# The expert layer of a decoder trunk: weights loaded as 7168-byte rows of one side at a time, in place of 3584-byte rows of gate and up in turn

## The reference, cut to what matters

```python
D_MODEL, SEQ, N_EXPERTS, TOP_K, D_FF_EXPERT = 1024, 256, 8, 2, 3584

def swiglu(h, w_gate, w_up, w_down):
    return (jax.nn.silu(h @ w_gate) * (h @ w_up)) @ w_down

def moe_swiglu(h, router_w, w_gate, w_up, w_down):
    logits = (tokens @ router_w).astype(jnp.float32)
    top_vals, top_idx = lax.top_k(logits, TOP_K)
    top_w = jax.nn.softmax(top_vals, axis=-1)
    combine = jnp.sum(jax.nn.one_hot(top_idx, N_EXPERTS) * top_w[..., None], axis=1)
    out = jnp.zeros_like(tokens)
    for e in range(N_EXPERTS):
        y = swiglu(tokens, w_gate[e], w_up[e], w_down[e])
        out = out + combine[:, e:e + 1] * y
```

## Time and profile before

| | us |
|---|---|
| median of three runs | 2023.57 |
| the profiled execution | 2022.8 |
| its span in the profile | 2021.0 |
| first hidden product of the first pass | 1154.81 |
| first hidden product of the second pass | 1261.51 |
| last down product of the last pass ends | 2007.45 |
| last store issued | 2016.67 |

### The profile page before, as it was taken

How to read it: one execution, slowest core, us unless ns; L and a number is a source line. 1 busy time by engine, 2 the same in 40 slices (tenths; PEclk the granted TensorE clock), 3 DMA queues, 4 the chain that set the end, 5 groups by cost and what they waited for, 6 DMA issues and landing times.

```text
span 2021.0 us, 67888 instructions
## 1 busy us (share of the span) xinstructions
PE 1945.3 (96%) x31760; PEld 1723.7 (85%) x31760; DVE 391.4 (19%) x945; ACT 273.1 (14%) x580; POOL 87.9 (4%) x174
## 2 busy tenths in 40 slices
PE   7999999999999999999999899999999999999997
PEld 7888888888777688888888799989998998989897
DVE  3335331110000133533311301001010001010001
ACT  1223214000000122222310000000000000000001
POOL 4010101000000001011000000000000000000000
PEclk9999999999999999999999899999999999999999
DMA  8413123467442141311346499999999999999996
GB/s 243 126 43 105 44 80 110 146 207 251 144 148 86 40 150 62 104 44 44 120 131 221 148 391 407 407 407 408 407 407 407 407 407 407 407 407 407 408 407 264
DMA packets 214765, 483.01 MB, mean 239 GB/s; under 512 B 11582, under 2 KB 110092, under 8 KB 214668
## 3 DMA queue, kind: packets, MB, share of 16 engines
q1 hardware_dynamic: 214668, 481.54, 64.0%
HBM read 480.46 MB, written 1.05 MB: 238 GB/s over the span
## 4 chain that ended last, share of the span: by engine, by line
PE 83%; DMA 6%; SPq 4%; DVE 3%; ACT 1%; issue 1%; POOL 0%; DVEq 0%; ACTq 0%
PE bank L640 32%; PE bank L627 18%; PE bank L1167 7%; DMA pool<-in_moe_w_down_dram 6%; PE bank L732 5%; PE bank L1090 4%; PE bank L1127 4%; SPq L2154 3%; PE bank L1106 3%; PE bank L688 2%; PE bank L1315 1%; SPq L2159 1%; PE bank L1053 1%; DVE pool L1834 0%; PE bank L1013 0%
## 5 line engine op out<-in xcount | busy, mean ns | idle before, releaser
L640 PE MATMUL bank<-pool 128*64 128x80 f32 x21504 | 757.6, 234 | 34.6 <-DMA pool<-in_moe_w_down_dram 26.8
L640 PEld LDWEIGHTS bank<-pool 128*64 128x64 f32 x21504 | 752.3, 138 | 41.3 <-DMA pool<-in_moe_w_down_dram 28.9
L627 PE MATMUL bank<-hnT,pool 128*128 128x256 f32 x1856 | 428.1, 384 | 0.4 <-DVE pool L1896 0.4
L627 PEld LDWEIGHTS bank<-hnT,pool 128*128 128x128 f32 x1856 | 346.5, 190 | 55.2 <-issue 8.8
L1167 PEld LDWEIGHTS bank<-hnT,pool 128*128 128x128 f32 x640 | 121.6, 190 | 23.3 <-issue 7.7
L1167 PE MATMUL bank<-hnT,pool 128*128 128x256 f32 x640 | 140.7, 379 | 0.0
L2054 DVE TENSOR_TENSOR pool<-pool,bank 128x320 f32<-128x320 f32 x32 | 15.6, 488 | 642.7 <-ACT pool L1601 642.7
L732 PEld LDWEIGHTS bank<-pool 64*64 64x64 f32 x3008 | 94.8, 135 | 17.2 <-issue 11.2
L1601 ACT ACTIVATE pool<-bank 128x320 f32<-128x320 f32 x32 | 14.0, 437 | 692.7 <-PE bank L640 692.7
L732 PE MATMUL bank<-pool 64*64 64x32 f32 (+2 forms) x3008 | 103.4, 221 | 2.6 <-DVE pool L1680 1.6
L565 POOL TENSOR_TENSOR pool<-pool,level_mask 128x256 f32<-128x256 f32 x72 | 51.9, 735 | 775.1 <-DVE pool L1756 495.1
(11 more groups left out here) (320 smaller groups left out, 1175.9 us busy)
## 6 DMA issues: line engine op xcount, KB each, us to landing
pool<-in_moe_w_up_dram SPq DMA_DIRECT2D x128, 896.0 KB, 16.6
pool<-in_moe_w_gate_dram SPq DMA_DIRECT2D x128, 896.0 KB, 16.6
pool<-in_w_in_dram SPq DMA_DIRECT2D x66, 1024.0 KB, 5.3
pool<-in_moe_w_down_dram SPq DMA_DIRECT2D x64, 1024.0 KB, 16.8
pool<-in_moe_w_down_dram SPq DMA_DIRECT2D x32, 1536.0 KB, 18.6
pool<-in_ffn_w_gate_dram SPq DMA_DIRECT2D x11, 1024.0 KB, 7.6
pool<-in_ffn_w_up_dram SPq DMA_DIRECT2D x11, 1024.0 KB, 5.5
pool<-in_ffn_w_down_dram SPq DMA_DIRECT2D x11, 1024.0 KB, 5.0
```

The lines of the kernel that those rows point to most:

```text
L627: ins = mm(ps[:, s * T:(s + 1) * T], w[:, k, (j + s) * P:(j + s + 1) * P], hnT[:, k, :], start=(k == 0), stop=(k == KD - 1))
L640: ins = mm(bank[rows, cs], w[:, rows], rhs, start=start, stop=stop, skip_group_check=True)
```

## The change

A pass becomes 2 halves (NH) of 14 tiles (HT) in place of 4 rounds of 7. In a half, TensorE first goes through all of gate, eight slots, then through all of up in the same eight slots, then through down in two rounds of 7 tiles. A hidden slot now holds one k-tile by 14 tiles of one matrix: 1792 floats as before, but 128 rows of 7168 bytes. The 14 tiles lie in four parts of 4, 3, 4 and 3 tiles (PARTS) in the four banks B[2], B[3], proj[0], proj[1]. Gate fills them; ScalarE takes silu of each into the buffer sge, now twice as large; up then fills the same banks, and VectorE multiplies sge by them into heT, which still holds 7 tiles, so parts 2 and 3 are multiplied only once down's first round has read parts 0 and 1. One semaphore, hid_free, counts both ScalarE's and VectorE's releases. Down has six slots (DSLOTS), five of one tile and one of two. The wait of TensorE for the residual adds (sc_added) moves from the first round to ahead of the zero matmuls.

The order of SP's queue in a pass is written in one_pass: up of half 0; gate of half 1, slots 0 and 1; down round 1; gate of half 1, slots 2 to 7; up of half 1; down round 2; the next pass's gate, slots 0 and 1; down round 3; the next pass's gate, slots 2 to 7; its down round 0. Ahead of the first pass SP loads down round 0 and gate of half 0.

```diff
-SPLIT = 4
-HSLOT = 2 * FB * P
-KH = 4
+NH = 2
+HT = FT // NH
+HSLOT = HT * P
+PARTS = (range(0, 4), range(4, 7), range(7, 11), range(11, 14))
+DSLOTS = 6
...
-            lo = 2 * KH * HSLOT
-            return pool[:, lo + 2 * n * D:lo + min(2 * n + (3 if n == 2 else 2), FB) * D].rearrange("p (f n) -> p f n", n=D)
-
-        assert 2 * KH * HSLOT + FB * D <= MRING * SLOT
+            lo = KD * HSLOT
+            return pool[:, lo + n * D:lo + (FB if n == DSLOTS - 1 else n + 1) * D].rearrange("p (f n) -> p f n", n=D)
+
+        assert KD * HSLOT + FB * D <= MRING * SLOT and KD + DSLOTS <= MRING
...
+                hidden_banks = (B[2], B[3], proj[0], proj[1])
                 with pe.Fori(0, n_pass) as i:
                     pe.wait_ge(xg_ready, i * 2 + 2)
                     pe.wait_ge(selT_ready, i + 1)
+                    pe.wait_ge(sc_added, i * 4 + 4)
                     for half in range(2):
                         mm(B[4 + half][:, 0:4 * CAP], zeros[:, 0:P], zeros[:, :], start=True, stop=False,
                            skip_group_check=True)
...
+                    with pe.Fori(0, NH) as h:
+
+                        def hidden(side):
+
+                            for n in range(KD):
+                                pe.wait_ge(hid_loaded[n], i * (32 * NH) + h * 32 + side * 16 + 16 * (slot_count[n] + 1))
+                                for q in range(4):
+                                    if n == 0:
+                                        pe.wait_ge(hid_free, i * (8 * NH) + h * 8 + side * 4 + (ff_base + q + 1))
+                                    for f in PARTS[q]:
+                                        at = f - PARTS[q][0]
+                                        ins = columns_mm(hidden_banks[q], slice(at * CAP, (at + 1) * CAP),
+                                                         hidden_slot(n)[:, f * P:(f + 1) * P], xgT[:, n, :],
+                                                         start=(n == 0 and at == 0), stop=(n == KD - 1))
+                                    if n == KD - 1:
+                                        ins.then_inc(hid_mm, 1)
+                                if n < KD - 1:
+                                    ins.then_inc(hid_used, 1)
+
+                        def down(r):
+
+                            for f in range(FB):
+                                if f == PARTS[0][0] or f == PARTS[1][0]:
+                                    pe.wait_ge(hid_free, i * (8 * NH) + h * 8 + r * 2
+                                               + (ff_base + 8 + (1 if f == PARTS[0][0] else 2)))
+                                n, at = min(f, DSLOTS - 1), max(f - (DSLOTS - 1), 0)
                                 if at == 0:
...
+                                    pe.wait_ge(dwn_loaded[n], i * (16 * NR) + h * 32 + r * 16 + 16 * (slot_count[KD + n] + 1))
+                                for k in range(KD):
+                                    ins = columns_mm(B[4 + k // 4], slice(k % 4 * CAP, (k % 4 + 1) * CAP),
+                                                     down_slot(n)[:, at, k * P:(k + 1) * P], heT[:, f, :],
+                                                     start=False, stop=False)
+                                    if f == FB - 1 and k % 4 == 3:
+                                        ins.then_inc(dwn_mm, 1)
+                                if n < DSLOTS - 1:
                                     ins.then_inc(dwn_used, 1)
...
+                        with pe.Fori(0, 2) as side:
+                            hidden(side)
+                        with pe.Fori(0, 2) as r:
+                            down(r)
...
+                for h in range(NH):
+                    for q in range(4):
+                        lo, n = PARTS[q][0], len(PARTS[q])
+                        act.wait_ge(hid_mm, i * (8 * NH) + (hid_base + 8 * h + q + 1))
+                        A(sge[:, lo:lo + n, :], (B[2], B[3], proj[0], proj[1])[q][:, 0:n * CAP].rearrange("p (f n) -> p f n", f=n),
+                          ACT.Silu).then_inc(hid_free, 1)
...
+                    for h in range(NH):
+                        for q in range(4):
+                            lo, n, g = PARTS[q][0], len(PARTS[q]), q % 2
+                            v.wait_ge(hid_mm, i * (8 * NH) + (hid_base + 8 * h + 4 + q + 1))
+                            if q == 2:
+                                v.wait_ge(dwn_used, i * ((DSLOTS - 1) * NR) + ((DSLOTS - 1) * 2 * h + 4))
+                            if q == 3:
+                                v.wait_ge(dwn_mm, i * (2 * NR) + (down_base + 4 * h + 2))
+                            tt(heT[:, PARTS[g][0]:PARTS[g][0] + n, :], sge[:, lo:lo + n, :],
+                               (B[2], B[3], proj[0], proj[1])[q][:, 0:n * CAP].rearrange("p (f n) -> p f n", f=n),
+                               ALU.mult).then_inc(hid_free, 1)
+                        if h == 0:
                             places(i + 1)
...
-            def hidden_load(n, e, col):
-
-                w = (a["moe_w_gate"], a["moe_w_up"])[n % 2]
-                rows = slice(n // 2 * 2 * P, (n // 2 + 1) * 2 * P)
-                src = w[0, e, rows, col].rearrange("a (k p) n -> p (a k) n", p=P)
+            def hidden_load(n, e, side, h):
+
+                w = (a["moe_w_gate"], a["moe_w_up"])[side]
+                src = w[0, e, n * P:(n + 1) * P, h * HSLOT:(h + 1) * HSLOT].rearrange("a p n -> p (a n)")
                 sp_.dma_start(hidden_slot(n), src).then_inc(hid_loaded[n], 16)

-            def down_load(n, e, rows):
-
-                src = a["moe_w_down"][0, e, rows, :].rearrange("a (f p) n -> p (a f) n", p=P)
+            def down_load(n, e, r):
+
+                lo, hi = (r * FB + n) * P, (r * FB + (FB if n == DSLOTS - 1 else n + 1)) * P
+                src = a["moe_w_down"][0, e, lo:hi, :].rearrange("a (f p) n -> p (a f) n", p=P)
                 sp_.dma_start(down_slot(n), src).then_inc(dwn_loaded[n], 16)
...
+            for n in range(DSLOTS):
+                down_load(n, slice(0, 1), 0)
...
+                        hidden_load(n, slice(0, 1), 0, 0)
                         fetched.append(n)
...
-            def later_round(e, col, hid, dwn):
-
-                for n in range(2 * KH):
-                    sp_.wait_ge(hid_used, hid + (n + 1))
-                    hidden_load(n, bass.ds(e, 1), bass.ds(col, FB * P))
-                for n in range(3):
-                    if n < 2:
-                        sp_.wait_ge(dwn_used, dwn + 1)
+            def hidden_round(i, at, e, slots):
+
+                h, side = at // 2 % NH, at % 2
+                for n in slots:
+                    if n < KD - 1:
+                        sp_.wait_ge(hid_used, i * ((KD - 1) * 2 * NH) + ((KD - 1) * (at - 1) + n + 1))
                     else:
-                        sp_.wait_ge(dwn_mm, dwn * 2 + (down_base + 2))
-                    lo, size = down_rows(n)
-                    down_load(n, bass.ds(e, 1), bass.ds(col + lo, size))
-
-            def rest_of_pass(i, e):
-
-                with sp_.Fori(0, NR - 1) as j:
-                    later_round(e, j * (FB * P) + FB * P, i * (2 * KH * NR) + j * (2 * KH), i * NR + j)
+                        sp_.wait_ge(hid_mm, i * (8 * NH) + (hid_base + 4 * at))
+                    hidden_load(n, bass.ds(e, 1), side, h)
+
+            def down_round(i, at, e):
+
+                for n in range(DSLOTS):
+                    if n < DSLOTS - 1:
+                        sp_.wait_ge(dwn_used, i * ((DSLOTS - 1) * NR) + ((DSLOTS - 1) * (at - 1) + n + 1))
+                    else:
+                        sp_.wait_ge(dwn_mm, i * (2 * NR) + (down_base + 2 * at))
+                    down_load(n, bass.ds(e, 1), at % NR)
+
+            def one_pass(i, e, next_e):
+
+                hidden_round(i, 1, e, range(0, KD))
+                hidden_round(i, 2, e, range(0, 2))
+                down_round(i, 1, e)
+                hidden_round(i, 2, e, range(2, KD))
+                hidden_round(i, 3, e, range(0, KD))
+                down_round(i, 2, e)
+                if next_e is not None:
+                    hidden_round(i, 4, next_e, range(0, 2))
+                down_round(i, 3, e)
+                if next_e is not None:
+                    hidden_round(i, 4, next_e, range(2, KD))
+                    down_round(i, 4, next_e)

```

More of the change, by code:

```diff
@@ L2176, in _ @@
                     clear.append(ring)
-                for n in range(2 * KH):
+                for n in range(KD):
                     needs = [r for r in range(RING) if r * SLOT < (n + 1) * HSLOT and n * HSLOT < (r + 1) * SLOT]
                     if n not in fetched and all(r in clear for r in needs):
-                        hidden_load(n, slice(0, 1), slice(0, FB * P))
+                        hidden_load(n, slice(0, 1), 0, 0)
                         fetched.append(n)
-            assert len(fetched) == 2 * KH
+            assert len(fetched) == KD
```

95 lines of the change are left out of this document (9 added, 86 removed).

## The result

The changed kernel takes 2049.9 us (median of 4 runs, 2045.1 to 2052.0) against 2023.5 in the same comparison: ratio 1.0135, 95% interval 1.0118 to 1.0151. It is slower, as forecast, but by three times the forecast, and outside the range (2014 to 2042). The profiled span is 2049.3 us against 2021.0: 28.3 us more, where the sum said 9.2.

A forecast was written before the change was run, and what follows sets the result against it. Transfers were taken to bound the kernel, TensorE having about 6 us of slack a pass. Long rows' gain was outweighed by a 2.5 us stream pause each pass; with the first pass's +4.8 us, +9.2 us gave 2032.8, range 2014 to 2042.

The forecast's parts named there:

- the sum: Whole kernel: first pass +4.8 us, six passes of 109.1 and a last without the next gate's two slots; +9.2 us.
- T0: The end of a pass's last down product, from which the forecast counted both TensorE's work and the transfers.
- The first pass: Its last down product was forecast at 1257.6 against 1252.85 before, +4.8 us, with the queue empty for some 12 us.
- The packet price: Time of one 7168-byte row in the hidden loads, taken as 275 ns, bounds 268 and 281.
- the rival that rows bring nothing: Long rows cut or no better per byte in the hidden loads: +6.0 us more, 2038.8 us; chance 0.13.
- the one that the stream doesn't pause: Long rows pay and the stream doesn't pause: passes of 106.6 us, 2011 us in all; chance 0.13.
- From there the bytes bind to the end of the pass.: After down 1's data start: 35.2 us of hidden slots, 27.15 of tiles, 0.2, 0.5 and 2.23; the pass 109.1 us.
- The 2.1 us from rows 9: Delay from a load's issue into an empty queue until its data in effect flow, read after a pause: 2.1 us.
- The last pass: Taken as a 109.1 us pass less 4.4 us, for the next gate's two slots that it doesn't load.
- The pause itself: Stream dry at T0 + 41.5 until down 1's data at T0 + 43.8: 2.3 us, with another 0.2 following.
- TensorE's leg: From T0 through 16 hidden slots and down 0's first tile until down 1's data flow, loop ends included: 43.8 us.
- TensorE's price for loop ends: Register work of TensorE's loops and waits in a half: 0.3 us a pass, bounds 0 and 1.

The follow-up runs named there:

- e1_gate4: Against the changed kernel, SP's order alone: four slots of the second half's gate, in place of two, go out ahead of down round 1; 2013.9 us.
- e3_rows3584: Against the changed kernel, each hidden load split into two loads of 448 KB with 3584-byte rows; 2062.5 us.
- e7_double: Against the changed kernel, two sets of down slots, down rounds written out, loads in the order slots come free; 2092.8 us.
- e6_unrolled: Against the changed kernel, TensorE's two inner loops (side and round) written out; 2245.5 us.

## Why the prediction was wrong

**What held.** The bound and the mechanism: SP's queue holds six freed gate slots behind down 1, the stream runs dry once a pass, and this costs more than the long rows bring. SP's first load of down 1 was predicted at T0 + 41.7 (43.8 less 2.1); it went out at 1411.91, 41.7 us after 1370.2. That this is exact is partly luck: TensorE took 9.07 us between the passes (8.66 in the sum), and SP issued 0.1 us after the tile was used (0.45 in the sum). The first pass's queue was empty from about 1183 to 1190, where 1180 to 1192 was forecast. The packet price was taken as 275 ns; two microseconds with only long rows have 116 of them beside 12 completions:

```profile
DMA packets 128, 0.83 MB, mean 416 GB/s; under 512 B 12, under 2 KB 12, under 8 KB 128
...
q1 hardware_dynamic: 128, 0.83, 100.3%
```

16 x 2000 / 116 = 276 ns. Full windows have 416 to 421 GB/s, more than the 412 forecast. That speaks against the rival that rows bring nothing; the one that the stream doesn't pause is false by the dip.

**The step that failed** is the one behind the pause: "From there the bytes bind to the end of the pass." It takes the full rate from the first byte of down 1 on, in every pass. It was short in three places, and they make up 19.0 us of the difference of 19.1:

- Passes 2 to 7, 110.84 against 109.07 forecast, +10.6 us. Down 1 was to land 11.9 us after its first issue (2.1 + 9.25 + 0.5). It landed at 1425.4, 13.5 us after: the loads are issued one at a time, as TensorE releases tiles, into an empty queue, which then moves 287 GB/s and not the 405 of a full one. The 2.1 us from rows 9 were taken once, but the queue stays shallow for the whole round. From there on the bytes did bind: down 3's last slot landed 52.8 us after down 1's, where the sum has 53.3, and in between the stream moved 417 GB/s. Told by the stream, the same pass is 104.6 us of transfers and 5.9 us missing, where the sum had 106.6 and 2.5: the pause was sized at less than half, and the faster stream hid 2 us of that.
- The last pass, from the last down product of the pass before to its own, 111.5 against 104.7, +6.9 us. I took off 4.4 us because it doesn't load the next gate. The bytes did not bind (286 GB/s from 2020 to 2031 us); TensorE, its clock and the reload of down's last slot did. The chain of the last pass in the changed kernel:

```profile
1933.28 39.28 PE bank L642 x1120
...
1972.71 7.51 DMA pool<-in_moe_w_down_dram
...
1980.27 43.13 PE bank L642 x1184
...
2023.56 8.00 DMA pool<-in_moe_w_down_dram
...
2031.60 4.08 PE bank L642 x64
```

39.3 us of matmuls, a load of 7.5, 43.1 of matmuls, a load of 8.0, and 64 matmuls at the low clock: no row of the stream's rate in it. The 43.1 us have a low stretch too; the same work takes 42.0 in the other passes. So 2.8 of the 6.9 us are the clock (1.1 and 4.08 less 2.43), by these rows. In e1_gate4, without the pause, the last pass took 108.8 us, and passes 4 to 7 105.7: there too nothing is queued ahead of down 3 in the last pass. The last slot of a down round is loaded only after all of the round before, so it can stand in the chain in each half.
- The first pass ends at 1259.1 against 1257.6, +1.5 us, though its first hidden product starts 0.9 us earlier than before (1153.92). Its timeline:

```profile
1169.47 33.20 PE L642 MATMUL bank<-pool 128*64 128x80 f32 x921 [2.70 <-issue]
1203.81 2.44 PE L642 MATMUL bank<-pool 128*64 128x80 f32 x64 [1.14 <-DMA pool<-in_moe_w_down_dram]
1206.65 39.23 PE L642 MATMUL bank<-pool 128*64 128x80 f32 x1120 [0.41 <-issue]
1249.00 10.10 PE L642 MATMUL bank<-pool 128*64 128x80 f32 x224 [3.12 <-DMA pool<-in_moe_w_down_dram]
```

One issue gap of 2.70 us (2.4 taken), then waits of 1.14 and 3.12 us for down 1 and down 3, the last followed by 10.10 us for 224 matmuls.

The pause itself was also too small: 2.5 us forecast, 5.3 us missing by the windows from 1408 to 1422. Of these 3.8 us lie before 1414.0, where data of down 1 were to flow, and 1.5 behind it, in the slow start just told. The start of down 1's data was right, so the stream ended sooner than T0 + 41.5; it faded from 1409 to 1411. I had counted from the moment when the last down slot of the pass before has landed less 0.5 us. In the records of the changed kernel, 4096-byte packets of that slot and 7168-byte packets of the next load overlap from 1365.0 to 1367.3: the 16 engines are some 2.3 us apart, and while the last of them finish one load, others are already in the next. So the stream was further in the mean than the landing says, by about 1.2 us as an estimate from these rows. No run tests that this is the cause. In the sum this changes nothing, since TensorE's leg sets the start of down 1: the 5.9 us of stream and the late landing are two accounts of one loss. It matters for how much cover a pause needs: four slots, where the forecast pause of 2.5 us would have asked for three or four.

The clock was no term at all. Passes 1 to 7 have a wait of about 3.2 us at down 3 and with it 3.4 or 6.8 us at 1.2 GHz. In passes with 3.4 us the chain goes past it, through the reload of the last down slot; in the two with 6.8 it goes through the slow matmuls. Two pieces of the chain, of passes 3 and 5:

```profile
1467.60 10.65 DMA pool<-in_moe_w_down_dram
...
1691.51 10.79 PE bank L642 x224
```

The two with 6.8 us took 111.3 and 111.7 us. Passes with the same wait for down 1 (1.21 and 1.72 us against 1.25 and 1.70) and 3.4 us of low clock took 110.5 and 111.1, so it adds 0.8 and 0.6 us there. With the 2.8 us of the last pass that is some 4 of the 19.1 us, an estimate from these rows; no run changes the clock alone.

TensorE's price for loop ends was taken at 0.3 us a pass. Its pace went from 34.8 to 35.1 ns (44.92 us for 1280), 0.8 us in 2688, and there is a gap of 0.36 us between halves. On the leg where the 0.3 was used, 928 matmuls took 32.5 us where the sum has 32.3: it was the right order.

The experiments show the order as the cause of the loss: with the same loops, rows, slots and bytes, two numbers in SP's queue are worth 36 us, more than the 26 that the change lost.

## What to carry to other kernels

When one queue feeds two rings of slots, its order fixes how much lies behind the load that has to wait for the slowest release; count the transfers ahead of that load against the time until its slot is free, in both directions: too few and the stream stops, too many and the reader waits, frees its slots late, and the stream stops behind the load. Here the right number was four of eight, one slot to either side costs 16 us, and an edit in one half moved the pause to the other, so the numbers are to be set together. When a change makes the stream faster, look again for what binds: a loop that was bound by bytes, with 6 us to spare on TensorE, became bound in its first half by TensorE and the one load that waits for a whole round, and in the last pass in both halves.

## What the runs showed of the hardware

- A queue that was empty and is fed load by load moved 287 GB/s in windows where full ones move 405 to 421 (changed kernel, 1413 to 1419 us).
- The 16 DMA engines of one stream were about 2.3 us apart (changed kernel, 4096-byte packets of one load and 7168-byte packets of the next overlapping from 1365.0 to 1367.3 us).
- Rows of 7168 bytes ran at 276 ns a packet in a window of 2 us and at 416 to 421 GB/s over full windows (changed kernel), those of 3584 bytes at 405 to 409, in loads of 896 KB (before) and of 448 KB (e3_rows3584) alike.
- Seven waits of TensorE of 3.1 to 3.2 us each came with 3.4 or 6.8 us at 1.2 GHz (changed kernel); of the ten waits of 2.11 to 2.13 us before the change three did.
- TensorE's loop of 672 pairs of weight load and matmul (a half of the changed kernel, a round of the one before) ran with 0.02 MB of code loads from 1262 to 2010 us in each. With 896 and 1344 pairs (e7_double, e6_unrolled) the kernel fetched 1.05 and 3.15 MB more, and TensorE stood for 46 and 155 us, and for 40 us more at the zero matmuls in each.
